# Latent attention's low parts on GpSimd, the query's factor in the root, and GpSimd's program by layer

## The reference, cut to what matters

```python
def latent_attention(c_q, c_kv, k_r, pos, cq_g, ckv_g, w_uq, w_ukv, q_g, k_g, out_g):
    q = (rms_norm_2(c_q, cq_g) @ w_uq).reshape(b, s, 4, 64 + 32)
    kv = (rms_norm_2(c_kv, ckv_g) @ w_ukv).reshape(b, s, 4, 64 + 64)
    k_nope, v = kv[..., :64], kv[..., 64:]
    k = concatenate([k_nope, broadcast(k_r)], -1)      # 96 wide
    q, k = rms_norm_2(q, q_g), rms_norm_2(k, k_g)      # x * rsqrt(mean(x*x) + 1e-6) * g
    q, k = rope on the last 32 of each
    logits = (q @ k.T) * 96 ** -0.5, masked by chunks of 64
    o = softmax(logits) @ v
    return rms_norm_2(o, out_g)
```

## Time and profile before

| | us |
|---|---|
| runs: lowest, median, highest | 3174.09, 3176.36, 3176.57 |
| the profiled execution's own time | 3174.81 |
| span of its profile | 3173.0 |
| TensorE matmuls busy | 3069.1 |
| DVE busy | 1644.8 |
| ScalarE busy | 1434.9 |
| GpSimd busy | 736.7 |

### The profile page before, as it was taken

The page is one execution under the profiler, slowest core; times in us unless marked ns, Lnnn a source line. Parts: engine busy times, 40 slices in busy tenths (PEclk is TensorE's granted clock), DMA queues, the critical chain, the costliest instruction groups (busy, mean ns, idle before and its releaser), DMA issues.

```text
span 3173.0 us, 43952 instructions
## 1 busy us (share of the span) xinstructions
PE 3069.1 (97%) x13727; PEld 2430.3 (77%) x13727; DVE 1644.8 (52%) x2441; ACT 1434.9 (45%) x2100; POOL 736.7 (23%) x508
## 2 busy tenths in 40 slices
PE   8999999999999999999999989999999988999998
PEld 6888888788887777888867767788887776778887
DVE  6544445575665977574657573511125756441113
ACT  4333333443333675343356764522345666542224
POOL 2333323100000000000023213244443220334444
PEclk9999999999999999999999999999999999999999
DMA  5333322333333232433222112133332220223334
GB/s 160 95 104 93 88 81 73 95 114 99 97 93 93 60 106 80 135 96 96 75 65 67 59 37 67 47 93 93 98 119 69 57 66 21 67 73 93 93 93 132
DMA packets 490394, 273.00 MB, mean 86 GB/s; under 512 B 9550, under 2 KB 479766, under 8 KB 489848
## 3 DMA queue, kind: packets, MB, share of 16 engines
q1 hardware_dynamic: 485576, 264.45, 29.0%
q10 hardware_dynamic: 4656, 6.58, 0.6%
HBM read 267.69 MB, written 12.21 MB: 88 GB/s over the span
## 4 chain that ended last, share of the span: by engine, by line
issue 56%; PE 30%; POOL 11%; DVE 2%; ACT 1%; POOLq 0%; ACTq 0%; DMA 0%; DVEq 0%
PE acc L753 9%; PE acc L754 9%; PE acc L759 8%; POOL s_w_lo L722 5%; POOL s_w_lo L721 5%; PE acc L756 1%; PE wide L785 1%; PE misc L754 0%; PE misc L753 0%; PE misc L759 0%; DVE s_sc L2610 0%; PE wide L753 0%; POOLq L111 0%; PE wide L754 0%; ACTq L1670 0%
## 5 line engine op out<-in xcount | busy, mean ns | idle before, releaser
L753 PE MATMUL acc<-s_h_hi,s_w_hi 128*128 128x512 f32 (+1 forms) x1920 | 787.8, 410 | 15.5 <-DVE s_h_lo L3053 9.2
L754 PE MATMUL acc<-s_h_lo,s_w_hi 128*128 128x512 f32 (+1 forms) x1920 | 753.2, 392 | 0.0
L721 POOL TENSOR_TENSOR s_w_lo<-s_raw,s_w_hi 128x512 fp32r<-128x512 f32 x212 | 274.9, 1297 | 2020.9 <-ACT s_w_hi L1623 2020.0
L759 PE MATMUL acc<-s_h_hi,s_w_lo 128*128 128x512 f32 (+1 forms) x1680 | 659.4, 393 | 0.0
L1623 ACT ACTIVATE s_w_hi<-s_raw 128x1024 fp32r<-128x1024 f32 x386 | 409.3, 1060 | 386.1 <-DVE s_x L3308 210.8
L753 PEld LDWEIGHTS acc<-s_h_hi,s_w_hi 128*128 128x128 f32 x1920 | 363.3, 189 | 115.6 <-issue 19.9
L754 PEld LDWEIGHTS acc<-s_h_lo,s_w_hi 128*128 128x128 f32 x1920 | 363.7, 189 | 87.5 <-issue 12.3
L759 PEld LDWEIGHTS acc<-s_h_hi,s_w_lo 128*128 128x128 f32 x1680 | 317.6, 189 | 73.1
L704 POOL TENSOR_TENSOR s_w_lo<-s_raw,s_w_hi 128x1024 fp32r<-128x1024 f32 x80 | 191.5, 2394 | 406.2 <-ACT s_w_hi L1623 404.6
L722 POOL TENSOR_TENSOR s_w_lo<-s_raw,s_w_hi 128x512 fp32r<-128x512 f32 x212 | 279.0, 1316 | 0.0
L753 PE MATMUL acc<-s_hid_hi,s_w_hi 128*128 128x512 f32 x704 | 278.1, 395 | 0.0
(11 more groups left out here) (498 smaller groups left out, 5416.4 us busy)
## 6 DMA issues: line engine op xcount, KB each, us to landing
s_raw<-w_ff SPq DMA_DIRECT2D x128, 512.0 KB, 4.0
s_raw<-ffn_w_up SPq DMA_DIRECT2D x96, 512.0 KB, 3.9
s_raw<-attn_w_qkv SPq DMA_DIRECT2D x72, 512.0 KB, 3.8
s_raw<-ffn_w_down SPq DMA_DIRECT2D x48, 512.0 KB, 4.0
s_raw<-w_in SPq DMA_DIRECT2D x48, 512.0 KB, 4.0
s_raw<-lru_w_in SPq DMA_DIRECT2D x16, 512.0 KB, 4.0
s_raw<-w_out SPq DMA_DIRECT2D x16, 512.0 KB, 4.0
s_bd<-bias_by_head SPq DMA_DIRECT2D x24, 256.0 KB, 5.0
```

The source lines that it names most:

```text
L721: pool.tensor_tensor(w_lo_b[s][:, 0:h, :], raw_b[s][:, 0:h, :], w_hi_b[s][:, 0:h, :].bitcast(F32), ALU.subtract)
L753: mm(out, ahi, bhi, start=start, stop=False, **kw)
L754: mm(out, ahi, blo, start=False, stop=False, **kw)
L759: mm(out, alo, bhi, start=False, stop=stop, **kw)
```

## The change

Keys' and queries' low parts move from DVE to GpSimd, with semaphores of their own (`mla_hi`, `mla_lo`). For that GpSimd's loop over four units becomes a loop over the two layers with all units written out: 30 units, the eight low parts, 74 units; 4 more follow the loop. DVE waits for the two low parts of the head before, before it scales the next key and query. The factor 96 ** -0.5 of the query leaves the two copies and goes into the reciprocal root: Ln takes the sum of squares with scale 1 and bias 96 x 1e-6, from a second column of `eps`, so the root comes out 96 ** -0.5 times what it was.

```diff
-        eps = sb("eps", [P, 1])
+        eps = sb("eps", [P, 2])
...
             count.second_ring()
-            with count.loop((LAYERS * UNITS_LAYER + AHEAD_2) // RING_B,
-                            "hi_split unit_ready") as i:
-                for _ in range(RING_B):
+            def units_by_halves(n):
+                for _ in range(n):
                     unit_by_halves()
+            def latent_los():
+                for h in range(HEADS_2):
+                    for (hi, lo), src in ((mla_k[h % 2], kr[0:MLA_W, :]), (mla_q[h % 2], tn[0:MLA_W, 0, :])):
+                        pool.wait_ge(sems["mla_hi"], count("mla_hi"))
+                        pool.tensor_tensor(lo, src, hi.bitcast(F32), ALU.subtract).then_inc(sems["mla_lo"], 1)
+                        pool.wait_ge(sems["mla_lo"], count("mla_lo"))
+            before_latent = len(UNITS_2) + 4 + 2 + 2
+            with count.loop(LAYERS, "hi_split unit_ready mla_hi mla_lo"):
+                units_by_halves(before_latent)
+                latent_los()
+                units_by_halves(UNITS_LAYER - before_latent)
+            units_by_halves(AHEAD_2)
...
                 def mla_scores(h):
-                    pe.wait_ge(sems["hn_lo"], count("hn_lo", 2))
+                    pe.wait_ge(sems["mla_lo"], count("mla_lo", 2))
...
-                    fn(dst, misc[0:rows, 0:n], ACT.Ln, bias=eps[0:rows, 0:1], scale=1.0 / features).then_inc(sems["misc_act"], 1)
+                    fn(dst, misc[0:rows, 0:n], ACT.Ln, bias=eps[0:rows, 0:1] if features else eps[0:rows, 1:2],
+                       scale=1.0 / features if features else 1.0).then_inc(sems["misc_act"], 1)
...
-                    fn(mla_k[h % 2][0], kr[0:MLA_W, :], ACT.Copy).then_inc(sems["hn_hi"], 1)
-                    act.wait_ge(sems["hn_hi"], count("hn_hi"))
+                    fn(mla_k[h % 2][0], kr[0:MLA_W, :], ACT.Copy).then_inc(sems["mla_hi"], 1)
+                    act.wait_ge(sems["mla_hi"], count("mla_hi"))
...
-                    fn(mla_q[h % 2][0], tn[0:MLA_W, 0, :], ACT.Copy, scale=MLA_W ** -0.5).then_inc(sems["hn_hi"], 1)
-                    act.wait_ge(sems["hn_hi"], count("hn_hi"))
+                    fn(mla_q[h % 2][0], tn[0:MLA_W, 0, :], ACT.Copy).then_inc(sems["mla_hi"], 1)
+                    act.wait_ge(sems["mla_hi"], count("mla_hi"))
...
-                head_rstd(MLA_W, MLA_W)
+                head_rstd(None, MLA_W)
...
-            nc.vector.memset(eps[:], EPS).then_inc(sems["zeroed"], 1)
+            nc.vector.memset(eps[:, 0:1], EPS)
+            nc.vector.memset(eps[:, 1:2], MLA_W * EPS).then_inc(sems["zeroed"], 1)
...
-                def mla_lo(h):
+                def mla_scaled(h):
+                    if h:
+                        dve.wait_ge(sems["mla_lo"], count("mla_lo", 2))
                     dve.wait_ge(sems["hn_rstd"], count("hn_rstd", 2))
...
-                    head_lo(mla_k[h % 2][1], kr[R, :], mla_k[h % 2][0])
-                    head_lo(mla_q[h % 2][1], tn[R, 0, :], mla_q[h % 2][0], MLA_W ** -0.5)
```

More of the change, by code:

```diff
@@ L279, in build_program @@
             "hn_sq hn_rstd hn_norm hn_hi hn_lo om_full po_full po_freed a_mid rot_full "
-            "l_sum mla_norm mla_ln kr_in rope_done mla_sq l_abs l_done z_full a_exp sq32 ".split())
+            "l_sum mla_norm mla_ln mla_hi mla_lo kr_in rope_done mla_sq l_abs l_done z_full a_exp sq32 ".split())
         sems = {n: ctx.enter_context(nc.semaphore(n)) for n in names}
@@ L1595, in _ @@
             with count.loop(LAYERS,
-                            "mla_sq acc_freed acc_full h_lo hid_lo hn_lo hn_sq m_lo misc_act misc_dve kr_in o_lo om_full "
+                            "mla_sq mla_lo acc_freed acc_full h_lo hid_lo hn_lo hn_sq m_lo misc_act misc_dve kr_in o_lo om_full "
                             "l_sum p_ready po_freed po_full rot_full ss_ready stat_full unit_ready v_turned wide_freed "
@@ L2405, in _ @@
             with count.loop(LAYERS,
-                            "mla_sq a_exp acc_freed acc_full exp_done h_hi hi_split hid_hi hid_lo hn_hi hn_norm hn_rstd "
+                            "mla_sq mla_hi a_exp acc_freed acc_full exp_done h_hi hi_split hid_hi hid_lo hn_hi hn_norm hn_rstd "
                             "hn_sq kr_in l_abs l_done m_hi misc_act mla_ln mn_in nmax_ready o_hi om_full po_freed pt_hi raw_B0 "
@@ L3170, in layer @@
                 mla_values()
-                mla_lo(0)
+                mla_scaled(0)
                 head_norm([(yo[:, 5, :], od[:], 0)], "sb_out_g_2")
@@ L3192, in layer @@
                     if h < HEADS_2 - 1:
-                        mla_lo(h + 1)
+                        mla_scaled(h + 1)
                     else:
@@ L3197, in layer @@
                         turned_a(q)
+                count("mla_lo", 2)
                 ys(range(3, 7))
@@ L3317, in _ @@
             with count.loop(LAYERS,
-                            "mla_sq a_mid acc_freed acc_full bd_cut bd_in exp_done h_hi h_lo hid_hi hid_lo hn_hi hn_lo hn_norm "
+                            "mla_sq mla_lo a_mid acc_freed acc_full bd_cut bd_in exp_done h_hi h_lo hid_hi hid_lo hn_hi hn_lo hn_norm "
                             "hn_rstd kr_in l_done l_sum m_hi m_lo misc_dve mla_norm mn_in nmax_ready o_hi o_lo "
```

## The result

After the change the median of ten runs is 3181.61 us (3178.45 to 3185.18), against 3174.53 us of ten runs of the kernel before in the same comparison (3172.05 to 3177.41): a ratio of 1.0023, with the interval 1.0014 to 1.0033, so **+7.1 us**. A second measurement, with 11 and 27 runs, gave 1.0017 (1.0008 to 1.0026), +6.0 us. The kernel is slower, by about twice the +3.2 us of the forecast. The median lies inside the forecast's range of 3174.0 to 3184.0, and the two differences lie on either side of the 0.2% (6.4 us) that it took as the bound between no change and slower. The profiled execution took 3180.50 us around its span, against 3174.81 before.

What follows compares the result with a forecast made beforehand. TensorE, busy 97% of the span, was taken as the bound. Later scores, +0.45 us in heads 1 and 2 and +0.6 in head 3, gave +3.0 over two layers, rounded to +3.2: 3176.36 + 3.2 = 3179.6 us, range 3174.0 to 3184.0.

Steps and rivals of the forecast that it cites:

- The gate and the distance: Heads 1 to 3: low parts hold back TensorE's scores; on GpSimd the scores start 0.6 us later.
- rival A's first half: GpSimd's subtractions take 0.97 us with 96 rows, so scores don't move: 3176.4 us; chance of the whole rival 0.22.
- What heads 1 and 2 absorb: Slack before the first exponential takes about 0.15 us of the 0.6 us delay, leaving +0.45 us per head.
- The clock: TensorE's clock falling at heads 1 and 2: 2.3 us each, four falls 9.2 us, 3188.8 us; a rival, chance 0.07.
- a granted clock below 1 before head 3: Sign listed as showing the forecast wrong: TensorE's clock below full in the latent stage ahead of head 3.
- Rival A's clock gain: Head 3's clock fall moves behind the scores, returning 2.3 us per layer: 3175.0 us; chance of the whole rival 0.22.
- DVE's time: DVE gets back 1.64 us per head, but its later work does not move: taken as 0.
- the shared port: DVE and GpSimd blocking each other in SBUF while low parts are made: 0, at most 6.6 us.
- rival C's collisions: Engine collisions at all six scores, 6.6 us, giving 3186 us; chance of the whole rival 0.08.
- The cover for the jump: At the layer's turn, GpSimd's 3.07 us idle time hides the long jump behind unit 104: cost 0.
- L1420 released by L2914 still: Sign listed as wrong: the first score product's wait still released by DVE's turned weights, not by GpSimd's subtraction.
- A GpSimd gap of more than 3 us at the layer's turn: Sign listed as showing the forecast wrong: GpSimd idle over 3 us where its program passes to the next layer.

Runs made afterwards that it cites:

- e2: The changed kernel with the low parts of keys and queries back on DVE: 3173.97 us, ratio 0.9998 to the kernel before.
- e5: The changed kernel with the key's low part made twice in every head: 3194.79 us, ratio 1.0064 to the kernel before.
- e0: The changed kernel run once more, unaltered, beside later runs: 3180.70 us, ratio 1.0017 to the kernel before.
- e4: The changed kernel with five unread matmuls ahead of the scores in heads 1 and 2: 3180.25 us, ratio 1.0019 to the kernel before.
- e8: The changed kernel with unread matmuls ahead of the scores, five in heads 1 and 2, fifteen in head 3: 3176.04 us, ratio 1.0007 to before.
- e1: The kernel before with only GpSimd's program written out by layer, no low part moved: 3174.92 us, ratio 1.0001.
- e3: The changed kernel with only the key's low part on GpSimd, the query's back on DVE: 3177.03 us, ratio 1.0007 to the kernel before.
- e6: The kernel before with twelve unread matmuls ahead of head 3's scores: 3171.98 us, ratio 0.9990.
- e9: The changed kernel with only the query's low part on GpSimd, the key's back on DVE: 3174.87 us, ratio 1.0001 to the kernel before.
- e10: The changed kernel with only the query's low part on GpSimd, plus twelve unread matmuls ahead of head 3's scores: 3171.56 us, ratio 0.9989 to before.

## Why the prediction was right and where it was wrong

- **The forecast's own time: in part luck.** 3179.6 us is only 2.0 below the measured 3181.61, because the median of three runs on which it was built (3176.36) lay 1.8 us above that of ten (3174.53). The effect was forecast as +3.2 and measured as +7.1 and +6.0.
- **The gate and the distance: right.** GpSimd's two subtractions in a row replaced DVE's two. 2.94 us was worked out for copy to scores (1874.26 to 1877.2), 2.93, 2.91 and 2.89 were measured. The 0.08 and 0.16 us of the waits and the 0.1 us to TensorE (0.13 measured) all held; 1.30 and 1.27 us for 96 partitions against 1.29 for 128. That fells rival A's first half (time by partitions). Head 0 loses nothing, as forecast: its parts are ready at 1858.72, 3.4 us ahead of its scores. e2 (undone: 0) and e5 (more: more) show the cause from both sides.
- **What heads 1 and 2 absorb: too high by 0.1 us each.** "Costs its own length less about 0.15 us" read the first exponential's idle of 0.15 us as slack. But in after, where DVE's maximum comes early, ScalarE still leaves 0.11 us at this place, between the root's end at 1879.79 and the exponential at 1879.90, and no releaser is named. So only about 0.04 us was slack. The term measures 0.56 x 6 = 3.4 us, against 3.0.
- **The clock: the step that failed.** "The idle time ahead of the scores doubles in heads 1 and 2", "1.2 is nearer the first": so a fall was priced (2.3 us; 2.4 measured in layer 2's head 1 of after) but left out of the sum, with 0.07 for four falls and nothing for one. That one fall is what the sum lacks in the profile of after; "a granted clock below 1 before head 3" was a sign of being wrong, and it came. Over all runs the clock's part is 1.9 us by the fillers, and 2.6 to 3.7 if all of the loss beside the starts' 3.4 is put down to it, which isn't shown. Two things go beyond the prediction's picture. A fall can come ahead of the wait, as in e0, e4 and e8, with nothing that TensorE did differently before it, and its price depends on its place: 2.4 us in the scores, 0 ahead of them in e0. In before, e1, e2, e3, e6, e9 and e10 the window of layer 2's head 1 has 1.00. A clock that falls in some places and some runs belongs in the sum as an expected cost, chance by price.
- **Rival A's clock gain**, head 3's fall moving behind the scores, did not come. In layer 1 the score at 1901.77 still has 0.47 us, the lower level, and the fall got longer. In layer 2 the first score has 0.32 us, full clock, but the fall comes right behind it (0.59 over 2677 to 2685), and from there to the next weights it is 26.85 us against 26.91: 0.06 us back, and not 2.3.
- **DVE's time, its new wait, the factor in the root, GpSimd's layout, the shared port: 0 each, right.** e1 and e2 show it for the root and the layout. The new wait is in neither; e9 has it, for one low part, and costs nothing (1.0001), and ScalarE's idle time ahead of the key's copy is 0.84 us with it and without it. For the port: the first three pieces of L2930 in head 1, which run beside GpSimd's two subtractions, take 0.29, 0.42 and 0.56 us, and none of the 64 takes over 0.69, as before, so rival C's collisions are absent. The cover for the jump was thinner than written: GpSimd idled 3.33 us there in e1 and 3.70 in e2, over the 3.07, came 0.33 and 0.71 us late, and only TensorE's 6.6 us of distance hid it. In after it was 3.06, and GpSimd on time:

```profile
2379.97 1.30 POOL L721 TENSOR_TENSOR s_w_lo<-s_raw,s_w_hi 128x512 fp32r<-128x512 f32 x1 [3.06 <-ACT s_w_hi L1637]
2389.20 0.50 PE L767 MATMUL acc<-s_h_hi,s_w_hi 128*128 128x512 f32 x1 [1.63 <-POOL s_w_lo L722]
```

- **Signs that misled.** The wait of L1434 was to name GpSimd, and "L1420 released by L2914 still" was listed as a sign against. It does name DVE, though DVE was 1.4 us early. Of several semaphores of one wait the view puts down one that had long been given; who was last is read from the ends of the instructions. "A GpSimd gap of more than 3 us at the layer's turn" could not tell anything: the kernel before has 3.07 there.
- **Open.** Why the clock falls in or ahead of layer 2's head 1 in all four profiles with both low parts on GpSimd (after, e0, e4, e8; in e5 only behind its longer wait), and in none of the others, is not settled: the idle times just ahead are the same in layer 1 (1.47, then 1.22 and 1.23 us), and in three of the four the fall precedes the first wait that the change made longer in that layer. Nor is it shown that in after's own profile the 1.23 us brought it. e4 shows that filling the last 1.2 us is not enough; filling further ahead, behind the wait of 1.46 us for the scaled weights of head 0, was not tried.

## What to carry to other kernels

Moving work to an idle engine pays only if the chain through it gets shorter; here 2 x 1.28 + 0.16 us in a row replaced 0.69 + 0.13 + 0.69 on the path, and the freed engine had nothing to do earlier. Where the bound engine idles just before a chain, count the idle time twice: once as a later start, once as a chance that its clock falls for the work behind it. Idle time that can't be removed can be filled: twelve matmuls that nobody reads, in a gap of 3 us, gave 2.7 us. It is worth trying only where the clock falls in or behind that gap: five in gaps of 1.2 us gave nothing (e4), and where the clock was already down they held the scores back by 0.9 us.

## What the runs showed of the hardware

- A filler in one idle stretch of 3 us, twice in the kernel, made it faster by 2.7 us though it adds 24 matmuls (e6).
- Idle stretches of 2.25 and 2.56 us ahead of the scores came with falls in heads 1 and 2 of both layers (e5). With 0.9 to 1.2 us the clock fell behind one of seven (after and e0); with 0.63 behind none of before's four.
- With the same idle times up to there, to 0.1 us, the clock fell near 2645 in e0, e4 and e8 and not in e2 and e9. A fall ahead of a wait cost nothing (e0), one in the chain behind it 2.4 us (after).
- GpSimd's subtraction takes the same time with 96 and with 128 partitions (1.26 to 1.30 us), where DVE's is 0.69 us.
- A DVE subtraction that starts 0.76 us into a GpSimd one costs 0.39 us more, and one at the same time as it 1.1 us more. In e3 0.53 us of GpSimd's instruction were left when DVE's began, and DVE lost 0.39.
